# A hybrid decoder layer on one core: probability rows scaled ahead of their turning, no spreading of sums, no stores of residual tiles

## The reference

```python
x = x + mix_out(attention(q, k, v), b * conv3(c * h))     # RMSNorm of each half, w_out
tok = rmsnorm(x)
top-1 of 4 groups, top-2 of 8 experts inside it, gates = softmax(top2) * p_group
hid = silu(xb @ w_gate[e]) * (xb @ w_up[e]);  y = hid @ w_down[e]
out = rmsnorm(x + sum over both choices of gate * y)
```

## Time and profile before

| | us |
|---|---|
| median of 3 runs (1078.28 to 1081.5) | 1078.99 |
| the profiled execution | 1078.28 |
| its span, first to last instruction | 1076.2 |
| TensorE busy | 1047.2 |
| VectorE busy | 448.6 |
| ScalarE busy | 274.0 |
| GpSimd busy | 130.3 |

### The profile page before, as it was taken

One profiled execution on the slowest core, in us unless ns is written; L12 is line 12 of the kernel. 1 busy time (PEld: TensorE's weight loads), 2 busy tenths in 40 slices (PEclk: granted clock), 3 DMA queues, 4 the chain that ended last, 5 costly groups with the idle time before them and its releaser, 6 DMA issues.

```text
span 1076.2 us, 19505 instructions
## 1 busy us (share of the span) xinstructions
PE 1047.2 (97%) x8020; PEld 681.9 (63%) x8020; DVE 448.6 (42%) x1104; ACT 274.0 (25%) x596; POOL 130.3 (12%) x167
## 2 busy tenths in 40 slices
PE   7999999999999999999999999999999999999887
PEld 6899999999966777888744433444344344443333
DVE  5414646333147768888854421222111111111156
ACT  7312211110117874322121111111111111111114
POOL 1001121002100000001012121120211211121010
PEclk9999999999999999999999999999999999999999
DMA  7215776244353526114999999999999999999987
GB/s 253 84 40 155 169 179 163 70 137 138 118 187 121 167 66 240 60 59 157 400 414 400 408 420 420 419 421 420 417 420 420 418 419 419 419 419 417 421 341 296
DMA packets 112286, 298.94 MB, mean 278 GB/s; under 512 B 44002, under 2 KB 68730, under 8 KB 87298
## 3 DMA queue, kind: packets, MB, share of 16 engines
q1 hardware_dynamic: 62786, 249.19, 58.5%
q0 software_dynamic: 14960, 40.03, 10.7%
q10 hardware_dynamic: 34448, 8.42, 3.5%
HBM read 280.58 MB, written 32.07 MB: 291 GB/s over the span
## 4 chain that ended last, share of the span: by engine, by line
PE 81%; SPq 8%; DMA 4%; DVE 4%; issue 2%; ACT 1%; DVEq 0%; ACTq 0%; POOLq 0%
PE psum L1355 16%; PE psum L956 9%; PE psum L958 8%; PE psum L957 8%; PE psum L1413 8%; SPq L819 7%; PE psum L1369 5%; DMA expert_w<-in_w_up 3%; PE psum L1108 3%; PE psum L1396 2%; PE psum L1110 2%; PE psum L1109 2%; PE psum L1339 2%; PE psum L1055 2%; PE psum L1049 1%
## 5 line engine op out<-in xcount | busy, mean ns | idle before, releaser
L1355 PE MATMUL psum<-expert_w,xT 128*64 128x512 f32 x512 | 229.1, 600 | 4.8 <-DMA expert_w<-in_w_up 4.6
L1357 PE MATMUL psum<-expert_w,xT 128*64 128x512 f32 x512 | 229.2, 600 | 0.0
L956 PE MATMUL psum<-h_hi,w_hi 128*128 128x344 f32 (+2 forms) x576 | 185.9, 323 | 3.0 <-DVE h_lo L1927 3.0
L958 PE MATMUL psum<-h_hi,w_lo 128*128 128x344 f32 (+2 forms) x576 | 184.0, 319 | 0.0
L957 PE MATMUL psum<-h_lo,w_hi 128*128 128x344 f32 (+2 forms) x576 | 183.9, 319 | 0.0
L1355 PEld LDWEIGHTS psum<-expert_w,xT 128*64 128x64 f32 x512 | 69.1, 138 | 143.2 <-issue 142.4
L1413 PE MATMUL psum<-expert_w,hT 128*64 128x512 f32 x512 | 116.9, 598 | 0.9 <-DVE hT L2563 0.9
L956 PEld LDWEIGHTS psum<-h_hi,w_hi 128*128 128x128 f32 x576 | 108.2, 188 | 6.2 <-DVE h_lo L1927 3.9
L958 PEld LDWEIGHTS psum<-h_hi,w_lo 128*128 128x128 f32 x576 | 108.2, 188 | 0.0
L957 PEld LDWEIGHTS psum<-h_lo,w_hi 128*128 128x128 f32 x576 | 108.2, 188 | 0.0
L2551 DVE TENSOR_TENSOR hid<-psum,silu_gate 64x512 f32<-64x512 f32 x32 | 21.9, 683 | 195.7 <-ACT silu_gate L1760 185.3
(11 more groups left out here) (336 smaller groups left out, 1370.9 us busy)
## 6 DMA issues: line engine op xcount, KB each, us to landing
expert_w<-in_w_gate SPq DMA_DIRECT2D x64, 1024.0 KB, 27.0
expert_w<-in_w_up SPq DMA_DIRECT2D x64, 1024.0 KB, 25.0
expert_w<-in_w_down SPq DMA_DIRECT2D x64, 1024.0 KB, 28.2
w_raw<-in_w_in SPq DMA_DIRECT2D x24, 512.0 KB, 5.5
y_tile<-y_rows SPq DMA_DIRECT2D x16, 512.0 KB, 13.6
kv<-in_cache_k POOLq DMA_DIRECT2D x24, 256.0 KB, 5.2
kv<-in_cache_v POOLq DMA_DIRECT2D x24, 256.0 KB, 4.3
x_tile<-in_x_prompt SPq DMA_DIRECT2D x8, 512.0 KB, 5.7
```

Source lines behind the costliest of these rows:

```text
L956: mm(ps, wh[:, k, :], h_hi[:, k, cols], start=(k == 0), stop=False)
L958: ins = mm(ps, wl[:, k, :], h_hi[:, k, cols], start=False, stop=(k == KD - 1))
L1355: mm(bank(0)[0:HEAD, :], xT[:, k, 0:HEAD], up[:, k, :], start=(k == 0), stop=(k == KD - 1), skip_group_check=True)
L1357: ins = mm(bank(0)[HEAD:P, :], xT[:, k, 0:HEAD], gate[:, k, :], start=(k == 0), stop=(k == KD - 1), skip_group_check=True)
```

## The change

The probabilities are multiplied by the reciprocals of their sums while they still stand in rows, where a sum is one number for each partition: rows 0 and 1 (query tile e = 0) by GpSimd, rows 2 and 3 by VectorE. So `spread_sums` goes, `copy_weight` and `divide` too; ScalarE copies the weighed values to `qT` itself (`take_values`). Turning comes three iterations after the scores and weighing four, the loops run one iteration longer, and the fourth projection group moves into them. There are three sets of score rows instead of two, and each row is a tile of its own; three of them lie where the sample's rows were, so `mask(2)` waits for the stores of these. The copy of the sample's sums moves to two places, one of which holds the router's weights later; so SP waits for it before it loads them. The stores of residual tiles go; the sums of the experts are written to tiles of their own (`totals`), and `xres` stays as it is.

```diff
                                                for i in (1, 2, 3)]
-s_held = at("sample_held", SROW, [512])
+s_held = [at("sample_held0", SROW + 12 * SPAN, [P]), at("sample_held1", MISC + 32768, [512 - P])]
 pack = Pack(WEI, WEI + 16384)
-sm = [pack(f"scores{s}", [4, SPAN]) for s in range(2)]
-weight = [pack(f"row_weight{s}", [2 * P]) for s in range(2)]
+sm = [[pack(f"scores{s}_{x}", [SPAN]) for x in range(4)] for s in range(2)]
+sm += [[pack("scores2_3", [SPAN])]]
+sm[2] = [at(f"scores2_{x}", SROW + 4 * SPAN * x, [SPAN]) for x in range(3)] + sm[2]
 v_far = at("v_far", WEI + 16384, [2, STRIDE, DA])
...
     sp.dma_start(gffn, a["norm_ffn"].partition_broadcast(P)).then_inc(router_in, 16)
+    sp.wait_ge(sample_held, 2)
     sp.dma_start(wr, a["w_router"]).then_inc(router_in, 16)
...
-    sp.wait_ge(res_out, 16 * NT)
     sp.wait_ge(first.sent, 16 * (NE - LAST))
...
             _, part, kind, at = units[g]
-            pe.wait_ge(exped, 4 * n + (2 * at + 2 if kind == "near" else 4))
+            if kind == "far" or at == 0:
+                pe.wait_ge(scaled_early, 2 * n + 2)
+            if kind == "far" or at == 1:
+                pe.wait_ge(scaled_late, 2 * n + 2)
             if g >= 3:
...
                         ins = nc.tensor.transpose(unit_psum(g)[:, k * P:(k + 1) * P],
-                                                  sm[n % 2][:, 2 * at + h, far + j * P:far + (j + 1) * P], ident)
+                                                  sm[n % 3][2 * at + h][:, far + j * P:far + (j + 1) * P], ident)
                         k += 1
...
                         ins = nc.tensor.transpose(unit_psum(g)[0:keys, k * P:(k + 1) * P],
-                                                  sm[n % 2][:, 2 * e + h, at * P:at * P + keys], ident)
+                                                  sm[n % 3][2 * e + h][:, at * P:at * P + keys], ident)
                         k += 1
             ins.then_inc(pT_ready, 1)
-
-    def spread_sums(n):
-
-        pe.wait_ge(rl_ready, n + 1)
-        if n >= 1:
-            pe.wait_ge(attended, n)
-        else:
-            pe.wait_ge(sample_held, 1)
-        for e in range(2):
-            for h in range(2):
-                mm(bank(7)[DH * h:DH * (h + 1), (2 + e) * P:(3 + e) * P],
-                   rl[:, n % 2, 2 * e + h:2 * e + h + 1].broadcast_to([P, DH]), ident,
-                   start=True, stop=True, skip_group_check=True)
...
         if n == 0:
+            pe.wait_ge(sample_held, 1)
             pe.wait_ge(v_in, 16)
+        else:
+            pe.wait_ge(attended, n)
         for e in range(2):
...
     pe.wait_ge(s_attn, 1)
-    for n in range(NSTEP + 3):
-        if 2 <= n < NSTEP + 2:
-            turn_probs(n - 2)
+    for n in range(NSTEP + 4):
+        if 3 <= n < NSTEP + 3:
+            turn_probs(n - 3)
         if n == 1:
...
                 project(1, *group_order[1][0], k)
-        if n >= 3:
-            spread_sums(n - 3)
-            weigh_values(n - 3)
+        if n >= 4:
+            weigh_values(n - 4)
         if n > NSTEP:
...
-    for n in range(MA):
-        project(1, *group_order[1][3], n)
     for pair in range(4):
...
-    def copy_weight(n):
+    def take_values(n):
+
+        i, m = steps_of[n]
         act.wait_ge(pv_done, n + 1)
-        if n >= 2:
-            act.wait_ge(attended, n - 1)
-        nc.scalar.copy(weight[n % 2], bank(7)[:, 2 * P:4 * P]).then_inc(weight_ready, 1)
+        nc.scalar.copy(by_class(qT[:, m, 2 * i * P:2 * (i + 1) * P], "c"), by_class(bank(7)[:, 0:2 * P], "k")
+                       ).then_inc(attended, 1)
...
         if n >= 4:
-            act.wait_ge(attended, n - 3)
+            act.wait_ge(rl_ready, n - 3)
         for r in range(4):
             act.wait_ge(masked, 4 * n + r + 1)
-            p = sm[n % 2][:, r, 0:width(steps_of[n][0], r // 2)]
+            p = sm[n % 3][r][:, 0:width(steps_of[n][0], r // 2)]
             nc.scalar.activation(p, p, ACT.Exp, bias=neg_n[:, n % 2, r:r + 1], scale=-1.0,
...
-    for n in range(NSTEP + 4):
-        if n >= 4:
-            copy_weight(n - 4)
+    for n in range(NSTEP + 5):
+        if n >= 5:
+            take_values(n - 5)
         if n == 2:
...
             bring_sample()
-        if 2 <= n < NSTEP + 2:
-            copy_pT(n - 2)
+        if 3 <= n < NSTEP + 3:
+            copy_pT(n - 3)
         if 1 <= n < NSTEP + 1:
...
             dve.wait_ge(attention_in, 16)
-        if n >= 2:
-            dve.wait_ge(pT_ready, first_unit[n - 1])
+        if n == 2:
+            dve.wait_ge(out_misc, 16 * 4)
+            dve.wait_ge(q_out, 16)
+        if n >= 3:
+            dve.wait_ge(pT_ready, first_unit[n - 2])
         for r in range(4):
...
             dve.wait_ge(s_ready, 4 * n + (r + 1 if i else 4))
-            vec.tensor_tensor_reduce(sm[n % 2][:, r, 0:w], score_psum(i, e, h)[:, 0:w],
+            vec.tensor_tensor_reduce(sm[n % 3][r][:, 0:w], score_psum(i, e, h)[:, 0:w],
                                      amask[:, e, SPAN - w:SPAN], -1.0, -NEG, ALU.add, ALU.min,
...
         dve.wait_ge(exped, 4 * n + 4)
+        if n >= 2:
+            dve.wait_ge(scaled_early, 2 * (n - 1))
+            dve.wait_ge(scaled_late, 2 * (n - 1))
         vec.reciprocal(rl[:, n % 2, :], lsum[:, n % 4, :]).then_inc(rl_ready, 1)
-
-    def divide(n):
-
-        i, m = steps_of[n]
-        dve.wait_ge(pv_done, n + 1)
-        dve.wait_ge(weight_ready, n + 1)
-        vec.tensor_tensor(by_class(qT[:, m, 2 * i * P:2 * (i + 1) * P], "c"), by_class(bank(7)[:, 0:2 * P], "k"),
-                          by_class(weight[n % 2], "k"), ALU.mult).then_inc(attended, 1)
+        dve.wait_ge(rl_ready, n + 1)
+        for r in range(2, 4):
+            x = sm[n % 3][r][:, 0:width(steps_of[n][0], r // 2)]
+            vec.tensor_scalar(x, x, rl[:, n % 2, r:r + 1], None, ALU.mult).then_inc(scaled_late, 1)
...
     for n in range(NSTEP + 4):
-        if n >= 4:
-            divide(n - 4)
-        if n == NSTEP + 2:
-            residual_both(0, group_order[0])
         if n == ROOT_AT + 1:
...
             invert_sums(n - 2)
-            copy_pT(n - 2)
+        if 3 <= n < NSTEP + 3:
+            copy_pT(n - 3)
+        if n == NSTEP + 2:
+            residual_both(0, group_order[0])
         if n < NSTEP:
...
         w = rows(t)
-        x = xres[0:w, t, :]
-        return vec.scalar_tensor_tensor(out=x, in0=yt[t % NY][0:w, :], scalar=gates[0:w, c, t:t + 1], in1=x,
-                                        op0=ALU.mult, op1=ALU.add)
+        total = totals[t][0:w, :]
+        return vec.scalar_tensor_tensor(out=total, in0=yt[t % NY][0:w, :], scalar=gates[0:w, c, t:t + 1],
+                                        in1=total if c else xres[0:w, t, :], op0=ALU.mult, op1=ALU.add)
...
+    for n in range(NSTEP):
+
+        pool.wait_ge(rl_ready, n + 1)
+        for r in range(2):
+            x = sm[n % 3][r][:, 0:width(steps_of[n][0], r // 2)]
+            gp.tensor_scalar(x, x, rl[:, n % 2, r:r + 1], None, ALU.mult).then_inc(scaled_early, 1)
+
     def store_h2(p):
...
-    def store_residual(p):
-        t = turn[p]
-        gp.dma_start(res_d[P * t:P * t + rows(t), :], xres[0:rows(t), t, :]).then_inc(res_out, 16)
-
     for p in range(NT - 2):
         store_h2(p)
-        store_residual(p)
     pool.wait_ge(o_ready, 4 * (NT - 1))
...
             fetch(first, column_of_block(b + 1, gidx, gmid))
-        if b == 0:
-            store_residual(NT - 2)
-            store_residual(NT - 1)
         if b == 2:
```

37 lines of the change are left out of this document (18 added, 19 removed).

## The result

The changed kernel took 1073.08 us (median of 5 runs, 1071.71 to 1074.17) beside 1078.28 us of the kernel before in the same session (5 runs, 1077.65 to 1081.5): a ratio of 0.9945, with an interval of 0.9933 to 0.9957. That is 5.2 us saved by the medians and 5.9 by the ratio, where 8.2 were forecast. The profiled execution took 1071.71 us, the fastest of its five, with a span of 1069.9: 6.3 us of span less than before.

The account below looks back on a forecast made before the run. TensorE bounds the attention; DMA and TensorE are both nearly full in the weights' stretch. Attention with hand-over 5.7 us plus stores 2.5 saves 8.2: 1070.1 for the profiled execution, 1070.4 beside the median, range 1067.3 to 1075.5 us.

Parts of the forecast that it names:

- hand-over: Behind the attention: VectorE's lead over TensorE shrinks, so the wait for the router's weights grows by 0.9 us (0 to 1.5).
- likeliest case: Whole kernel: all terms hold, 8.2 us saved, 1069 to 1072.6 us; chance 0.53.
- spreading gone: Attention, TensorE: 16 spreadings of sums at 0.38 us each go, saving 6.1 us.
- first turnings: Attention's start: TensorE waits for GpSimd's scaled rows at the first turning only, costing 0.3 us (0 to 0.7).
- Step 1: Attention: no spreading between scores and weighing, iterations of 6.1 instead of 6.46 us, 6.1 us saved in all.
- Step 2: Attention's other engines: GpSimd multiplies 448 elements in 0.65 us, VectorE in 0.44; TensorE waits only at the first turning.
- Step 3: Attention's end: waits there go, 0.8 us gained; the router's weights wait grows by 0.9, to near 1.4 us.
- Step 4: Weights' stretch: two removed residual stores save 2.5 us of transfers; the only wait for weights falls from 4.6 to 2.1.
- the sign of being wrong that I had named: End of the weights' stretch: the forecast would be wrong if the last wait for weights grows.
- The dip of the clock after the last wait: After TensorE's wait for weights: its clock dip of 1.7 us may go too, giving 1068.7 us; chance 0.14.
- The transfers don't pay: Weights' stretch: the 2.5 us of removed stores are lost in the queues, giving 1072.9 us; chance 0.13.
- The mutual hold-up of VectorE and GpSimd: Attention: their multiplications wait for each other; at 0.5 us each the attention gains only 1.0, giving 1075.5; chance 0.13.

Follow-up runs that it names:

- a_spread: The changed kernel with the four small matmuls of the old spreading put back ahead of each step's weighing: 1079.39 us, ratio 1.0004 to the kernel before.
- a_wr: The changed kernel with VectorE's scaling of the router's weights moved ahead of tile 7's second pair of residual additions: 1072.08 us, ratio 0.9938 to the kernel before.
- a_stores: The changed kernel with the nine stores of residual tiles put back at their old places: 1074.32 us, ratio 0.9957 to the kernel before.
- b_nostores: The kernel before without its nine stores of residual tiles, nothing else changed: 1079.20 us beside 1079.24, ratio 1.0007.
- a_dve_alone: The changed kernel with GpSimd's 32 multiplications and the waits for them left out: 1072.53 us in one run.
- a_dve4: The changed kernel with all four rows scaled by VectorE and none by GpSimd: 1074.59 us beside 1079.06 of the kernel before, ratio 0.9951.

## Why the prediction was right, and where it was not

The direction is right, the place is the attention with its hand-over as said, and the time lies in the range, though 0.5 us outside the likeliest case (1069 to 1072.6); the gain was forecast at 8.2 us of the own execution and came to 6.3 of span. (The forecast of 1070.4 is 8.2 below 1078.6, a base between the 1078.3 and the 1079.0 that it gives; beside 1079.0 its sum makes 1070.8.) Term by term:

| term | forecast | measured | from |
|---|---|---|---|
| spreading gone | 6.1 | 7.0 | iterations of 6.02 for 6.46, and `a_spread` |
| first turnings | -0.3 | -1.8 | waits for GpSimd's rows |
| waits at the attention's end | +0.8 | +0.8 | 0.78 and 0.68 of the earlier trace rows, less 0.35 each, are not there any more |
| hand-over | -0.9 | -1.1 | 5.44 instead of 4.32 us |
| attention with hand-over | 5.7 | 5.3 (0.4 unplaced) | 93.74 instead of 99.04 us |
| stretch of the weights | 2.5 | 1.2, of it 0.1 to 0.5 by the stores; like kernels scatter by 2.0 | 502.96 instead of 504.13 us |
| after the last wait | 0 | -0.5; like kernels scatter by 2.0 | 68.03 instead of 67.53 us |

That 5.7 and 5.3 lie so close is luck in part: 0.9 too little for the spreading and 1.5 too little for the first turnings' wait stand against each other.

**Step 1** was mis-sized from below: I priced the removed instructions by the time from their start to the next line's, 0.38, and an iteration gives 0.44: 7.0 us and not 6.1.

**Step 2** bounded GpSimd's multiplication from the wrong row. I took 0.65 us for 448 elements, near the memset, because there is one input; it is 1.40 alone, which is above my upper bound of 1.04 from the two-input subtraction as well. The slope is (1.402 - 0.603)/320 = 2.5 ns an element, with 0.28 us to begin with. The Trainium skill, GPSIMD Engine Reference, section Engine selection, has work with one input roughly at line rate; these rows speak against it for a multiplication by a number per partition: the same row costs VectorE 0.45. That this cost only 1.8 us, and that only once, was forecast: the pair fits in an iteration, and the new wait is met one iteration ahead.

**Step 3** held: the waits at the end went, and the one for the router's weights, 0.55 us in the earlier trace rows, stands at 1.67 by the same kind of row, where 0.55 and 0.9 more, near 1.4, was said. VectorE starts tile 7 here, against TensorE's turning at 409.43:

```profile
406.19 1.54 DVE L2086 SCALAR_TENSOR_TENSOR xres<-psum,stat,xres 128x512 f32<-128x512 f32 x2
```

So its lead is 3.2 us where 3.5 was said. Most of that is a slip in the sum: 409.12 to 416.04 less the spreading (0.38) and a group (2.94) is 3.6 and not 3.75, which makes the lead 3.3 and the term about 1.1, as measured. That the wait can be moved away is shown by `a_wr`.

**Step 4 is the step that failed**: "That wait falls to 2.1, so all 2.5 us count." I took a mean DMA share of 1.01 over 504 us as proof that every byte pays. The two stores went through at a place where the loads have no free slot behind them, and what the DMA engines no longer carried there they spent idle. The last wait stays 4.6 us (and doesn't grow, the sign of being wrong that I had named), and a second one of 1.4 us comes up at 985 us, as TensorE is further ahead of the weights than before.

What shortened that stretch by the rest of its 1.2 us, if it is more than scatter, came from elsewhere; this is argued from four executions and no run isolates it. Before, TensorE waited 1.34 us until 554.78 for the gathered rows of block 1, and the granted clock is 0.72 of full speed in the 6 us from 554 on, so part of them at 1.2 instead of 2.4 GHz; neither is there in the changed kernel (1.00 in the 6 us at the same place):

```profile
554.00:560.00 6.00, 5.22 (x20) 2.39 (x22) 5.55 (x14) 0.96 (x2) 1.06 (x1) 0.72 1.01 424
584.00:594.00 10.00, 10.00 (x98) 4.77 (x88) 3.25 (x6) 2.24 (x5) 2.35 (x3) 1.00 0.99 392
```
```profile
548.00:554.00 6.00, 5.78 (x33) 2.86 (x33) 5.31 (x12) 0.92 (x2) 1.27 (x1) 1.00 1.01 418
576.30:586.30 10.00, 10.00 (x92) 4.73 (x86) 3.57 (x7) 2.24 (x5) 2.72 (x3) 1.00 1.02 425
```

(the kernel before, then the changed one, 6 us at that wait and 10 us some 30 us later). TensorE is then 8 us ahead instead of 5.4, slots come free earlier, and the DMA engines move 425 instead of 392 GB/s in the 10 us, 0.33 MB or 0.8 us. `a_stores`, which has the attention's change and the stores, moves 424 GB/s in the same 10 us (stretch 503.06 us), and `b_nostores`, which has neither, 390 in the ten from 584 on (503.68). The gather of block 1's rows lands 7.8 us after its issue in both kernels with the old attention, and 5.7 to 6.3 in most with the new one, but 7.5 in `a_dve_alone`; these runs don't tell why.

**The rivals.** The dip of the clock after the last wait didn't go, as TensorE waits as long as before. In the 6.33 us from the end of that wait on the mean granted clock is 0.65 where it was 0.73 (rows below, before and after), which is 0.08 x 6.33 = 0.5 us, the length by which the end grew; like kernels scatter by more there. "The transfers don't pay" came true, though its reasons (the queues, the row transfers) are not the cause; that its time, 1072.9, is within 0.2 us of the measured one is luck, as it leaves out the 1.2 us gained in the stretch, the 0.5 lost behind it and the 0.4 that the attention with its hand-over falls short. The mutual hold-up of VectorE and GpSimd exists, at 0.14 us instead of the 0.34 that it needed. The Trainium skill, SBUF — State Buffer, section Who interferes with whom, has the second engine wait for the whole of the other's instruction; here VectorE's pair of 448 takes 1.20 us beside a GpSimd instruction of 1.5 us that spans most of it, and 0.82 alone, so it is held for 0.38 and not for the whole. How the two share, no run here shows.

```profile
1008.67:1015.00 6.33, 6.33 (x22) 2.39 (x24) 0.00 (x0) 0.00 (x0) 0.00 (x0) 0.73 1.01 422
```
```profile
1001.87:1008.20 6.33, 6.33 (x20) 2.23 (x22) 0.00 (x0) 0.00 (x0) 0.00 (x0) 0.65 1.01 423
```

## What to carry to other kernels

A mean DMA share near 1 over a long stretch doesn't say that bytes count everywhere in it. Look at the place of the transfer in slices of a few us, and ask whether the queue has something to send next: behind a ring without free slots, removed bytes become idle time. Before 1 us in a stretch of one profiled execution is read as an effect, see how far kernels that have the same instructions there lie apart. Price a removed group of instructions by the iteration that gets shorter, or by a kernel that has only it put back, and an operation that an engine hasn't done yet by more than a neighbouring row: here both ends of the bound were too low. When a pipeline is made deeper, list what each helping engine does ahead of the first use; a split that waited for its load had stood behind the copies, and then stood ahead of them.

## What the runs showed of the hardware

- GpSimd's multiplication of SBUF by a number per partition takes 0.60, 1.08, 1.24 and 1.40 us for 128, 320, 384 and 448 elements: 2.5 ns an element and 0.28 us. VectorE's takes 0.45 for 448.
- The two beside each other: 0.09 to 0.13 us more for each of GpSimd's, 0.06 to 0.19 for each of VectorE's. One of GpSimd's beside three of VectorE's took 1.90 us, 0.5 more than alone.
- 2.1 MB of stores lengthened the weights' stretch by 1.25 us in one place and by 4.27 in another, 105 us later (one execution each; like kernels scatter by 2.0 us).
- Behind a wait of 2.35 us in the attention (`a_dve4`) TensorE's mean granted clock was 0.66 of full speed over 5 us; behind one of 1.60 us (the changed kernel) it stayed 1.00.
